# One hybrid encoder layer on one Trainium2 core: the selection's query norm applied behind its scores, and the down weights' rounding on ScalarE

## The reference

```python
def peer(h, w_q, g_q, sub_keys, u_tab, v_tab):
    ...
    q = rmsnorm((x @ w_q).reshape(T, PEER_HEADS, PEER_QDIM), g_q)
    q = q.reshape(T, PEER_HEADS, 2, PEER_QDIM // 2)
    sc = jnp.einsum('thpd,hpkd->thpk', q, sub_keys.astype(q.dtype)).astype(jnp.float32)
    s_top, i_top = lax.top_k(sc, PEER_TOPK)
    ...
        a = jnp.einsum('td,tkd->tk', xt, u).astype(jnp.float32)
        c = (gt * jax.nn.gelu(a, approximate=False)).astype(xt.dtype)
        return jnp.einsum('tk,tkd->td', c, vsel)
```

## Time and profile before

| | before |
|---|---|
| median of 3 runs | 4938.73 us (4936.74 to 4941.19) |
| the profiled execution | 4938.4 us |
| its span, first to last instruction | 4936.6 us |
| mean granted TensorE clock | 0.992 |
| TensorE matmuls busy | 4847.3 us (98%) |
| VectorE, ScalarE, GpSimd busy | 3243.0, 1497.5, 2832.4 us |

### The profile page before, as it was taken

The page is one execution under the profiler, slowest core; times in us unless marked ns, Lnnn a source line. Parts: engine busy times, 40 slices in busy tenths (PEclk is TensorE's granted clock), DMA queues, the critical chain, the costliest instruction groups (busy, mean ns, idle before and its releaser), DMA issues. The chain is left out here.

```text
span 4936.6 us, 78893 instructions
## 1 busy us (share of the span) xinstructions
PE 4847.3 (98%) x32224; PEld 4731.9 (96%) x32224; DVE 3243.0 (66%) x4242; ACT 1497.5 (30%) x2899; POOL 2832.4 (57%) x1650
## 2 busy tenths in 40 slices
PE   8999999999999999999999999999999999999998
PEld 8999999999998879999999999999999999999998
DVE  5777777773423534216577776667775898999955
ACT  4333333332423432102221226666662000000001
POOL 7200000003333435554277878999997999999976
PEclk9999999999999999999999999999999999999999
DMA  7333333335343536523344449999997888888853
GB/s 272 114 129 130 126 129 127 126 122 148 107 149 131 206 129 232 181 87 131 120 144 141 143 154 324 337 336 335 335 333 286 306 311 308 303 312 302 313 182 105
DMA packets 343208, 1013.07 MB, mean 205 GB/s; under 512 B 39728, under 2 KB 132112, under 8 KB 307232
## 3 DMA queue, kind: packets, MB, share of 16 engines
q1 hardware_dynamic: 165776, 526.23, 31.9%
q0 software_dynamic: 36864, 268.45, 14.5%
q10 hardware_dynamic: 140208, 213.34, 12.0%
HBM read 882.26 MB, written 126.76 MB: 204 GB/s over the span
## 5 line engine op out<-in xcount | busy, mean ns | idle before, releaser
L213 POOL TENSOR_SCALAR w_hi<-w_raw 128x1024 fp32r<-128x1024 f32 x678 | 782.7, 1154 | 1941.8 <-PE ps L745 1080.0
L216 POOL TENSOR_TENSOR w_lo<-w_raw,w_hi 128x1024 fp32r<-128x1024 f32 x678 | 1687.4, 2489 | 56.5
L243 PE MATMUL ps<-h_hi,w_hi 128*128 128x416 f32 (+1 forms) x3552 | 1053.5, 331 | 13.4 <-PEq L2007 3.3
L247 PE MATMUL ps<-h_hi,w_lo 128*128 128x416 f32 (+1 forms) x3552 | 1037.4, 327 | 0.0
L245 PE MATMUL ps<-h_lo,w_hi 128*128 128x416 f32 (+1 forms) x3552 | 1028.6, 324 | 0.0
L243 PE MATMUL ps<-ex_c_hi,w_hi 128*128 128x416 f32 x2048 | 719.2, 351 | 8.2 <-DVE ex_c_lo L2928 7.9
L247 PE MATMUL ps<-ex_c_hi,w_lo 128*128 128x416 f32 x2048 | 724.1, 354 | 0.0
L245 PE MATMUL ps<-ex_c_lo,w_hi 128*128 128x416 f32 x2048 | 716.0, 350 | 0.0
L243 PEld LDWEIGHTS ps<-h_hi,w_hi 128*128 128x128 f32 x3552 | 625.3, 189 | 22.1 <-issue 10.5
L245 PEld LDWEIGHTS ps<-h_lo,w_hi 128*128 128x128 f32 x3552 | 624.2, 189 | 6.3
L247 PEld LDWEIGHTS ps<-h_hi,w_lo 128*128 128x128 f32 x3552 | 621.9, 189 | 2.5
(11 more groups left out here) (364 smaller groups left out, 9243.8 us busy)
## 6 DMA issues: line engine op xcount, KB each, us to landing
w_raw<-weights SPq DMA_DIRECT2D x906, 512.0 KB, 4.0
up<-up_out ACTq DMA_DIRECT2D x128, 208.0 KB, 6.6
gate<-g_sb_g ACTq DMA_DIRECT2D x13, 2048.0 KB, 13.9
proj<-rows_out ACTq DMA_DIRECT2D x97, 272.0 KB, 2.8
ex_up<-up ACTq DMA_DIRECT2D x16, 832.0 KB, 7.1
ex_gate<-gate ACTq DMA_DIRECT2D x16, 832.0 KB, 17.2
sp_first<-proj ACTq DMA_DIRECT2D x48, 272.0 KB, 3.6
sp_first<-up ACTq DMA_DIRECT2D x15, 832.0 KB, 7.3
```

What stands on the lines that cost most here:

```text
L213: pool.tensor_scalar(self.whi[:, to, :], self.raw[:, slot, :], 1.0, 1.0, ALU.mult, ALU.mult).then_inc(self.hi_done, 1)
L216: pool.tensor_tensor(self.wlo[:, to, :], self.raw[:, slot, :], self.whi[:, to, :].bitcast(F32), ALU.subtract).then_inc(self.split_done, 1)
L243: pe.matmul(acc, hi, x, start=first, stop=False)
L247: mm = pe.matmul(acc, lo, x, start=False, stop=last)
```

## The change

It has two parts. **In the selection** the queries are no longer normalized before the scores. The gain goes into the keys (two scaled copies on ScalarE), the raw queries are the scores' weights, and the inverse root multiplies the scores as ScalarE copies them out, tile by tile. For that the sums are needed with tokens on the partitions: the squares become the weights and one column of ones the moving operand, five tiles with a column each. Root and reciprocal then run over 5 columns instead of 544. **In the expert sets** ScalarE rounds the down weights from piece 11 on; GpSimd keeps the subtraction. The roundings stand in ScalarE's list between the coefficients' copies and behind them.

```diff
@@ rest_of_piece, and a new helper below it @@
-        pool.tensor_tensor(self.wlo[:, slot, :], self.raw[:, slot, :],
-                           self.whi[:, slot, :].bitcast(F32), ALU.subtract).then_inc(self.split_done, 1)
+        to = self.halves_at(slot)
+        pool.tensor_tensor(self.wlo[:, to, :], self.raw[:, slot, :],
+                           self.whi[:, to, :].bitcast(F32), ALU.subtract).then_inc(self.split_done, 1)
+
+    def round_piece(self, act, i):
+        slot = i % RING
+        act.wait_ge(self.hi_done, i)
+        act.wait_ge(self.raw_loaded[slot], 16 * (i // RING + 1))
+        act.wait_ge(self.piece_used, i - RING + 1)
+        act.activation(self.whi[:, self.halves_at(slot), :], self.raw[:, slot, :], ACT.Copy).then_inc(self.hi_done, 1)
@@ stage_select: tiles and steps @@
-        q, qn, sq = sb("q", [P, KC, T]), sb("qn", [P, KC, T]), sb("sq", [P, KC, T])
-        std, rstd = sb("std", [P, T]), sb("rstd", [P, T])
-        keys = sb("keys", [P, 2, N_KEYS])
+        q, sq = sb("q", [P, KC, T]), sb("sq", [P, KC, T])
+        std, rstd = sb("std", [P, NT]), sb("rstd", [P, NT])
+        keys, scaled_keys = sb("keys", [P, 2, N_KEYS]), sb("scaled_keys", [P, 2, N_KEYS])
...
@@ stage_select, TensorE @@
             def sums(h):
                 pe.wait_ge(act_s.sem, act_s.at("sq", h))
-                for c in range(KC):
-                    for j, (t0, n) in enumerate(HALVES):
-                        mm = pe.matmul(ps[:, j, 0:n], core.ones, sq[:, c, t0:t0 + n], start=(c == 0),
-                                       stop=(c == KC - 1))
+                for tile, (t0, n) in enumerate(TILES):
+                    for c in range(KC):
+                        mm = pe.matmul(ps[0:n, 0, tile:tile + 1], sq[:, c, t0:t0 + n], core.ones[:, 0:1],
+                                       start=(c == 0), stop=(c == KC - 1))
                 mm.then_inc(*pe_s.did("sum"))
 
             def scores(h):
-                pe.wait_ge(keys_loaded, 16 * (h + 1))
                 if needed(h):
                     pe.wait_ge(act_s.sem, act_s.at("sc_s", h - 1))
-                pe.wait_ge(dve_s.sem, dve_s.at("qn1", h))
+                pe.wait_ge(act_s.sem, act_s.at("keys", h))
                 for tile, (t0, n) in enumerate(TILES):
                     for part in range(2):
                         at = 256 * (tile % 2) + part * N_KEYS
-                        mm = pe.matmul(ps[0:n, 2 + tile // 2, at:at + N_KEYS], qn[:, part, t0:t0 + n],
-                                       keys[:, part, :], start=True, stop=True)
+                        mm = pe.matmul(ps[0:n, 2 + tile // 2, at:at + N_KEYS], q[:, part, t0:t0 + n],
+                                       scaled_keys[:, part, :], start=True, stop=True)
@@ stage_select, ScalarE @@
             def square(h):
                 act.wait_ge(q_loaded, 16 * (h + 1))
                 act.activation(sq[:, :, :], q[:, :, :], ACT.Square).then_inc(*act_s.did("sq"))
+                act.wait_ge(keys_loaded, 16 * (h + 1))
+                for part in range(2):
+                    ins = act.activation(scaled_keys[:, part, :], keys[:, part, :], ACT.Copy,
+                                         scale=core.gain[:, G_PEER + part:G_PEER + part + 1])
+                ins.then_inc(*act_s.did("keys"))
 
             def root(h):
                 act.wait_ge(pe_s.sem, pe_s.at("sum", h))
-                act.activation(halves_of(std[:, :]), core.acc_view(0), ACT.Sqrt, bias=core.eps,
+                act.activation(std[:, 0:NT - 1], ps[:, 0, 0:NT - 1], ACT.Sqrt, bias=core.eps, scale=1.0 / PEER_HD)
+                act.activation(std[0:SHORT, NT - 1:NT], ps[0:SHORT, 0, NT - 1:NT], ACT.Sqrt, bias=core.eps[0:SHORT],
                                scale=1.0 / PEER_HD).then_inc(*act_s.did("std"))
 
             def head(h, last=False):
                 act.wait_ge(pe_s.sem, pe_s.at("scores", h))
                 if needed(h):
                     act.wait_ge(dve_s.sem, dve_s.at("rep", h - 1))
-                act.activation(sc[:, 0:8, :],
-                               ps[:, 2:4, :].rearrange("p b (u k) -> p (b u) k", k=N_KEYS),
-                               ACT.Copy).then_inc(*act_s.did("sc"))
-                act.activation(sc[0:SHORT, 8:10, :],
-                               ps[0:SHORT, 4, 0:2 * N_KEYS].rearrange("p (u k) -> p u k", k=N_KEYS),
-                               ACT.Copy).then_inc(*act_s.did("sc_s"))
+                act.wait_ge(dve_s.sem, dve_s.at("rstd", h))
+                for tile, (_, n) in enumerate(TILES):
+                    at = 2 * N_KEYS * (tile % 2)
+                    ins = act.activation(sc[0:n, 2 * tile:2 * tile + 2, :],
+                                         ps[0:n, 2 + tile // 2, at:at + 2 * N_KEYS].rearrange("p (u k) -> p u k", k=N_KEYS),
+                                         ACT.Copy, scale=rstd[0:n, tile:tile + 1])
+                    if tile == NT - 2:
+                        ins.then_inc(*act_s.did("sc"))
+                ins.then_inc(*act_s.did("sc_s"))
@@ stage_select, VectorE @@
-            def normalize(h):
+            def invert(h):
                 dve.wait_ge(act_s.sem, act_s.at("std", h))
-                if needed(h):
-                    dve.wait_ge(pe_s.sem, pe_s.at("scores", h - 1))
                 dve.reciprocal(rstd[:, :], std[:, :]).then_inc(*dve_s.did("rstd"))
-                dve.wait_ge(dve_s.sem, dve_s.at("rstd", h))
-                dve.wait_ge(q_loaded, 16 * (h + 1))
-                for c in range(KC):
-                    dve.scalar_tensor_tensor(qn[:, c, :], q[:, c, :], core.gain[:, G_PEER + c:G_PEER + c + 1],
-                                             rstd[:, :], ALU.mult, ALU.mult).then_inc(*dve_s.did(f"qn{c}"))
@@ stage_experts @@
+    ROUNDED = AT_DOWN + SET_PIECES + AHEAD
...
@@ stage_experts, GpSimd @@
-                core.split_piece(pool, i % RING, i, i // RING)
+                if i < ROUNDED:
+                    core.split_piece(pool, i % RING, i, i // RING)
+                else:
+                    core.rest_of_piece(pool, i % RING, i)
@@ stage_experts, ScalarE @@
+            def round_ahead(G, piece):
+                i = down_at(G) + AHEAD + piece
+                if ROUNDED <= i < N_PIECES:
+                    core.round_piece(act, i)
             for G in range(N_SETS):
                 for c in range(VSET):
                     s = VSET * (G % 2) + c
+                    if G >= 2:
+                        round_ahead(G - 1, c)
                     act.wait_ge(weighed, VSET * G + c + 1)
                     if needed(G - 1):
                         act.wait_ge(core.piece_used, down_at(G - 1))
                     act.activation(c_hi[:, s, :], c_all[:, c, :], ACT.Copy).then_inc(hi_done, 1)
+                for piece in range(VSET, SET_PIECES if G >= 2 else 0):
+                    round_ahead(G - 1, piece)
...
+            round_ahead(LAST, 0)
             act.activation(norm.std[:, 0:1], core.eps, ACT.Sqrt)
             for k in range(KD):
                 norm.square(act, k)
+                if k % 2:
+                    round_ahead(LAST, k // 2 + 1)
```

More of the change, by code:

```diff
@@ L2378, in stage_select @@
         pe_s = Steps(sem("pe"), ["sum", "scores"])
-        act_s = Steps(sem("act"), ["sc", "sc_s", "sq", "std", "e"], ["sq", "std"])
-        dve_s = Steps(sem("dve"), ["max1", "idx1", "rep", "max2", "idx2", "rstd", "qn0", "qn1", "cand", "bmax1",
+        act_s = Steps(sem("act"), ["sc", "sc_s", "sq", "keys", "std", "e"], ["sq", "keys", "std"])
+        dve_s = Steps(sem("dve"), ["max1", "idx1", "rep", "max2", "idx2", "rstd", "cand", "bmax1",
                                    "bidx1", "brep", "bmax2", "bidx2", "row", "col", "rank", "top_f", "over",
                                    "hot0", "hot1", "val0", "val1", "id0", "id1", "total", "inv", "gate"],
-                      ["rstd", "qn0", "qn1"])
-        normed = 3
+                      ["rstd"])
+        normed = 1
         block = ctx.enter_context(nc.Block())
@@ L2497, in _ @@
         def _(dve):
+            dve.memset(std[:, :], 1.0)
             dve.memset(sc[:, 8:10, :], 0.0).then_inc(cleared, 1)
@@ L2538, in head @@
                 if last:
-                    dve_s.skip("rstd", "qn0", "qn1")
+                    dve_s.skip("rstd")
                 else:
-                    normalize(h + 1)
+                    invert(h + 1)
                 shape = [P, NT, TOPK, TOPK]
@@ L2589, in head @@
                     dve.tensor_reduce(at(part), grid(part), AX_X, ALU.add).then_inc(*dve_s.did(f"id{part}"))
-                dve.wait_ge(act_s.sem, act_s.at("e", h) - (2 if last else 0))
+                dve.wait_ge(act_s.sem, act_s.at("e", h) - (3 if last else 0))
                 dve.tensor_reduce(total[:, :], e[:, :, :], AX_X, ALU.add).then_inc(*dve_s.did("total"))
@@ L2596, in head @@
                                             ALU.mult).then_inc(*dve_s.did("gate"))
-            normalize(0)
+            invert(0)
             rounds(dve, PEER_HEADS - 1, head)
```

## The result

The change makes the kernel slower by 6.9 us: 4946.58 us median (4940.80 to 4949.52, 20 runs) against 4939.68 (4931.15 to 4942.97, 20 runs), ratio 1.0014, 95% interval 1.0008 to 1.0020. Forecast were 4951.0, in a range of 4939.5 to 4957.0; that is +12.6 us from the profiled 4938.4, so the change costs little more than half of what was forecast. The profiled execution took 4947.5 us for a span of 4945.7, 9.1 more than the one before.

The account below looks back on a forecast made before the run. TensorE, busy 98% of the span, was taken as the bound. The profiled 4938.4 us plus 4.0 for the thin sums and 8.6 for falls of the clock gave 4951.0, the rounding 0; range 4939.5 to 4957.

Parts of the forecast that it names:

- VectorE's 58 us in the selection: Selection: VectorE loses 7.7 us a head, some 60 us of 370; TensorE never waited for it, so worth 0.
- keys' copy: Selection, ScalarE: two scaled copies of 128 keys per head, 0.39 us each.
- scores' copy: Selection, ScalarE: score copies of 256 columns, taken at 0.5 us each.
- The thin sums: Selection, TensorE: twenty one-column matmuls 0.112 us apart take 2.32 us against 1.82, +0.50 a head, +4.0 for eight.
- the seam: Selection: TensorE's stretch from the last big matmul's start to the next one's around the sums, 1.82 us before, 2.3 forecast.
- The Trainium skill's 25 ns for few columns: Selection sums: by this page twenty matmuls take 0.5 us, worth -10 us; the prediction held measured 0.112 us against it.
- The falls: Selection: the clock drops to half behind 5 of 8 heads' sums (8 x 8/11 = 5.8, rounded down), 1.71 us each, +8.6.
- seam only: Rival, selection: weight loads or the twenty columns hold the clock, no drops to half clock; 4942.4 us, chance 0.35.
- three pieces, 13.6 us, cover 1.06 + 2.46: gain 0, cost 0: Expert sets: pieces prepared ahead cover ScalarE's rounding (1.06 us) and GpSimd's remainder (2.46), so moving the rounding is worth 0.
- Set 26's copy: Expert set 26: ScalarE's copy of the sparse rows, behind the last rounding, ends 0.7 us before the transposes want it.
- work taken off VectorE and GpSimd can buy nothing: Whole kernel: TensorE's only wait for the weights' low halves is 1.1 us, so relieving these engines gains nothing directly.
- TensorE's pace doesn't depend on who works beside it: Expert sets: TensorE's matmuls keep 0.189 us at 91% GpSimd, so relieving GpSimd doesn't speed them.

Follow-up runs that it names:

- wide_ones: The whole change, but the sums of squares move 96 columns of ones instead of one, against the kernel before: 4942.67 us against 4939.27, ratio 1.0008.

## Why the prediction came out as it did

**Direction and place of the cost: right.** All of the cost is in the selection's sums and the falls behind them, and the steady sets last 36.27 us before and after. VectorE's 58 us in the selection bought nothing. ScalarE's groups landed where they were put: keys' copy 0.386 us (0.39), scores' copy 0.470 (0.5):

```profile
L2479 ACT ACTIVATE sel_sb_sc<-ps,sel_sb_rstd 128x256 f32<-128x256 f32 (+1 forms) x40 | 15.2, 470 | 14.2 <-PE ps L2421 14.2
L2462 ACT ACTIVATE sel_sb_scaled_keys<-sel_sb_keys,gain_sb 128x128 f32<-128x128 f32 x14 | 4.8, 386 | 0.0
L2522 DVE RECIPROCAL sel_sb_rstd<-sel_sb_std 128x5 f32<-128x5 f32 x8 | 1.5, 191 | 59.9 <-ACT sel_sb_std L2469 59.9
```

**The thin sums: mechanism right, size off by two.** "2.32 us against 1.82: +0.50 us a head, +4.0 us for eight" measured 2.18 against 1.82, and 0.25 a head, 2.0 for eight. The pace of 0.112 held. I hadn't seen that the first two start 0.03 us apart (0.08 us less than a step of the pace), and that behind the old sums the next big matmul but one came 0.39 us after the first instead of 0.19 (behind the new 0.29): the seam reached one matmul further than I measured it. The Trainium skill's 25 ns for few columns ("TensorE: Matmul & The Clock Gate", section "Back-to-back issue gap") agrees with the start of the second matmul (0.028 behind the first) and of the last ones with 32-wide weights (0.031), and not with the others, where the pace is 0.112.

**The falls: right, the price a little high.** Five forecast, five in each of four traces. That the number is met exactly is in part luck: the count of stops gave 5.8, and it was rounded down. Which heads fall differs from trace to trace. "5 x 1.71 = +8.6" was 5 x 1.56 = 7.8. Half of 3.41 us is lost only if full clock doubles the pace; big matmuls start 0.347 us apart at half clock and 0.189 at full, so 3.41 x (1 - 0.189 / 0.347) = 1.55. The rival "seam only", that there are no falls, is refuted by the change itself, with TensorE busy through each of them. The Trainium skill's section "HAM oscillation — how this bites in real kernels" ("TensorE: Matmul & The Clock Gate") tells of idle gaps alone, and this trace goes beyond it. Of the change and wide_ones, both busy, only the one that moves 96 columns keeps its clock.

**"three pieces, 13.6 us, cover 1.06 + 2.46: gain 0, cost 0": the gain that was put at nothing, and wasn't.** The cost was 0. GpSimd now waits for ScalarE and TensorE for neither:

```profile
L225 POOL TENSOR_TENSOR w_lo<-w_raw,w_hi 128x1024 fp32r<-128x1024 f32 x242 | 583.9, 2413 | 365.7 <-ACT w_hi L233 365.7
L2333 POOL DMA_INDIRECT ex_v_rows<-peer_v,sp_expert x126 | 133.1, 1056 | 19.2 <-issue 2.2
```

Set 26's copy ended 1.4 us before its transposes (0.7 forecast), as the DMA issues ran beside the rounding. But the gain wasn't 0: about 3 us in the sum of the sets, 4.5 at the entry into set 1 alone. Two steps led past it. The table of the sets began at 3790 us, 3 us behind the stop at 3786.61, which stands in rows 7 with its cause, VectorE's low halves. I took it there for an example of a stop, and from rows 3, which name only the wait for GpSimd's low halves, I said that work taken off VectorE and GpSimd can buy nothing. And "TensorE's pace doesn't depend on who works beside it" holds in the steady sets, but says nothing of VectorE, whose low halves GpSimd does hold up. Of the 7.9 us of waits for the coefficients' low halves in the trace before 5.5 are at the start of set 0, with and without the change; 2.4 were the ones to ask about.

So 4938.4 + 2.0 + 7.8 - 3 = 4945.2, beside 4946.6 measured. All three terms were off the same way, by 2.0, 0.8 and 3 us, together 5.8 too slow. That the forecast missed by 4.4 only is luck: the span ahead of the selection, where nothing was changed, was 1.4 us longer.

## What to carry to other kernels

Before trading wide matmuls for many with own weights and few columns, count what TensorE's list gets. Here each such instruction with 128-wide weights took 0.112 us, whether 1, 2 or 96 columns were moved, and eight stretches of 2.2 us cost 2.0 us by their length and 7.8 by falls of the clock. Splitting the stretch or filling it with idle columns ended the falls; halving the instructions did so and shortened it as well, at the price of rounded sums. Where two engines slow each other, look also at the entry of a stage, where one is late, and not only at its steady part.

## What the runs showed of the hardware

- A thin stretch of 2.2 us (twenty matmuls of one moving column) was followed by a fall of the clock in 20 of 32 cases over four traces; one of 1.1 us (ten of two columns) in none of 8, two of 1.0 and 1.3 us with 4.4 us of big matmuls between in none of 7, one of over 4 us in 8 of 8, and one of 2.5 us with 96 columns in none of 8.
- Matmuls with 128-wide float32 or float32r weights of their own start 0.112 us apart with 1, 2 or 96 moving columns; with 32-wide weights and one column 0.031.
- A fall of 3.41 us cost 1.56 us: the big matmuls start 0.347 us apart in it and 0.189 at full clock.
- VectorE's subtraction of 416 columns, 0.57 us alone, took up to 2.8 us beside GpSimd's; in the sets its mean fell from 1.53 to 0.91 us when GpSimd's roundings went.
- One trace of the kernel before had sets 2 to 25 0.6% shorter (36.05 us for 36.27) at the same granted clock of 1.00. What sets it apart stays open.
